# Feed-forward parts that multiply activations before they are normalised

## The chip, the cores and the metric

The kernel runs on one core of a Trainium2 chip. The metric is the device time of one execution in microseconds (us). PE is TensorE, PEld its weight loads, DVE is VectorE, ACT is ScalarE, POOL is GpSimd, SP is SyncE, which issues the loads from HBM.

## What is computed

Two blocks on 256 tokens of width 1024, each with two layers. The first block mixes 256 latent and 256 context tokens in layer 0; in layer 1 it computes outputs for the latent tokens alone. A layer of the first block ends in a modulated RMS norm and a feed-forward part, the block in an RMS norm. A layer of the second block is feed-forward, attention, feed-forward, each followed by a layer norm:

```python
def swiglu(u, w_ffn_in, w_ffn_out):
    gate, up = jnp.split(u @ w_ffn_in, 2, axis=-1)
    return (jax.nn.silu(gate) * up) @ w_ffn_out
...
    h = h + g2 * swiglu(modulate(rms_norm(h, norm2_w), sh2, sc2), w_ffn_in, w_ffn_out)
...
        x = layer_norm(ALPHA * x + 0.5 * swiglu_2(x, ffn1_w_in[l], ffn1_w_out[l]), ln_g[l, 0], ln_b[l, 0])
        mix = hybrid_mixer(x, cos, sin, mask, w_in[l], w_out[l], diff_lambda[l],
                           diff_subln_g[l], swa_sink[l], lambda_init)
        x = layer_norm(ALPHA * x + mix, ln_g[l, 1], ln_b[l, 1])
        x = layer_norm(ALPHA * x + 0.5 * swiglu_2(x, ffn2_w_in[l], ffn2_w_out[l]), ln_g[l, 2], ln_b[l, 2])
```

The hidden width is 2816, 22 tiles of 128.

## The kernel before

The program is written engine by engine, with semaphores between them; each engine runs its instructions in the order of the text. Activations lie transposed: `h` has 8 tiles (k = 0 to 7) of 128 features by tokens.

Weights come in **panels** of 128 x 2048 numbers (1 MB). Each panel is loaded into one of three `raw` buffers, then split into a high part `whi` (ACT, L569) and a rest `wlo` (L578: DVE takes 1280 of the 2048 columns, POOL 768). Activations are split the same way, into `xh` and `xl`. A product is three fp32r matmuls (L601 to L603): high x high, high weight x low, low weight x high. Every engine calls `step(p)` when it comes to panel p, and this splits panel p + 2; ACT's split waits until PE has used panel p - 1, whose buffer it takes.

A **feed-forward part** (`ffn`) has 33 panels. An input panel holds the gate and up weights of one hidden tile: 2 x 8 x 3 = 48 matmuls of 256 columns into one PSUM bank (bank 4 or 5; gate in columns 0 to 255, up in 256 to 511). An output panel holds two hidden tiles: 48 matmuls (L987 to L989) that accumulate into banks 0 to 3, which PE sets to zero at the start of the part (L962: 3 x 4 matmuls of 512 bf16 columns). Two input panels stand ahead of a loop whose body is input, input, output, input, input, output; a single output panel ends the part. An output panel takes the two tiles before the last two. For each tile ACT applies Silu to the gate (`sg`, L1838), DVE multiplies with up (`hidf`, L2522), ACT makes the high half (`hidh`, L1840), and DVE the low half (`hidl`, L2524).

There are seven parts. Two are in layer 0 of the first block. The five others, in the order of time: `("ffn", 1, 0)` after the output projection of layer 1; `ffn1` of layer 0 after the final norm (`"final"`); `ffn2` of layer 0 after the attention layer's projection (`("out2", 0)`); `ffn1` of layer 1 after `ffn2`; `ffn2` of layer 1 after `("out2", 1)`. They are called the first to the fifth part below.

Between two stages the norm stands on the path. For a layer norm PE sums `h` with a matrix of ones (L1523, 8 calls, two records each), ACT copies the mean, DVE subtracts it, ACT squares (L636), PE sums the squares (L628), ACT takes the root (L641), DVE the reciprocal (L652) and multiplies (L2937), ACT and DVE make the two halves (L2164, L2942), and PE starts the first tile, one k after the other. An RMS norm is the same without means. In the last loop turn of the first part DVE also computes the angles and lambda scalars of the second block (L2469 to L2500).

Of the kernel before, what the change touches and what calls it, by code (L numbers as in the profile page):

```python
# [21 lines left out]
P = 128  # L22
D, KD = 1024, 8
S, T = 256, 512
L = 2
# [17 lines left out]
PAR = {}  # L43
# [86 lines left out]
def program(nc, a, out, known):  # L130

    signals = {}
    with ExitStack() as stack:
# [36 lines left out]
        hid_hi, hid_lo = sem("hid_hi"), sem("hid_lo")  # L170
        gate_ready, merged = sem("gate_ready"), sem("merged")
# [143 lines left out]
        ytok2, _ = at(y_at + 14 * S * 4, "ytok2", [P, 2, D])  # L315
        ed, o = at(o, "ed", [P, 2, T])
        rc, o = at(o, "rc", [P, 2, S])
        sqs, o = at(o, "sqs", [P, 2, P])
        top = max(top, o)

        f2, _ = at(y_at, "f2", [P, 14, S])
        assert top <= nc.sbuf_usable_end, (top, nc.sbuf_usable_end)
# [333 lines left out]


# [120 lines left out]
        def _(pe):  # L778
# [176 lines left out]
            def ffn(tag, p0, t0, ops, last=False, fresh=None, evacuated=None, mids=None):  # L955

                fh, fl, cols = ops

# [4 lines left out]
                if evacuated is None:  # L963
# [15 lines left out]
                def output(p, per, it, pair_end, step, s_, final=False):  # L979
# [3 lines left out]
                    for j in range(2):  # L983
                        for n in range(8):
                            w0 = 1024 * j + P * n
                            dst = bank[n // 2][:, S * (n % 2):S * (n % 2) + S]
                            pe.matmul(dst, hi[:, w0:w0 + P], hidh[:, s_, j, :], start=False, stop=False, skip_group_check=True)  # L987
                            pe.matmul(dst, hi[:, w0:w0 + P], hidl[:, s_, j, :], start=False, stop=False, skip_group_check=True)  # L988
                            m = pe.matmul(dst, lo[:, w0:w0 + P], hidh[:, s_, j, :], start=False, stop=False, skip_group_check=True)  # L989
                            if final and j == 1 and n in (1, 3, 5):  # L990
                                m.then_inc(*pe_done.tick((tag, "acc", n // 2)))
                    m.then_inc(panel_used, 1)
# [11 lines left out]
                hidden(0, p0, 0, 0, t0, 0, fresh)  # L1004
                hidden(1, p0 + 1, 0, 0, t0 + 1, 0)
                if evacuated is not None:
                    pe.wait_ge(*dve_done.at(evacuated))
                    zero_banks()
# [2304 lines left out]
```

## Time and profile before

| | |
|---|---|
| median of 3 runs | 2973.78 us (2956.91 to 2979.4) |
| profiled execution | 2975.17 us, span of the instructions 2973.4 us |
| PE busy | 2815.5 us of the span |
| DVE, ACT, POOL busy | 1386.2, 1236.2, 1122.3 us |
| granted clock of TensorE, mean | 0.979 of full |

A matmul's record overlaps the next one's, so a busy PE is read from the spacing of starts, not from durations.

### The profile page before, as it was taken

What the parts mean: (1) busy time and instruction counts of PE and PEld (TensorE: products, weight loads), DVE (VectorE), ACT (ScalarE), POOL (GpSimd) and SP (SyncE); (2) the same over time, 40 slices, a digit from 0 to 9 for tenths busy, and PEclk for the clock granted to TensorE, in tenths of its full rate; (3) what the DMA queues carried; (4) which work ended last, traced back from release to release, by engine and by line L of the source; (5) the groups of instructions that cost most, each with busy time, mean ns of one, the idle gap of its engine ahead of it and who ended that gap; (6) DMA issues with size and microseconds to landing.
All of it is one profiled execution on the core that took longest, in us unless ns stands there. A gap on an engine that the chain in (4) does not pass through costs nothing. (4 is left out here: it accounts for less than half of the span.)

```text
span 2973.4 us, 53484 instructions
## 1 busy us (share of the span) xinstructions
PE 2815.5 (95%) x20993; PEld 2515.8 (85%) x20993; DVE 1386.2 (47%) x2415; ACT 1236.2 (42%) x1822; POOL 1122.3 (38%) x461
## 2 busy tenths in 40 slices
PE   7999999999999999899999998999889999988998
PEld 5667777788899999685889998998779989977898
DVE  4453543433633535536455435434754353466433
ACT  3321133433444545322455444444544444454443
POOL 1002021122455554110335454454526555543553
PEclk9998999999999999999999999999999999999999
DMA  6562352333466665210446565564326656622463
GB/s 221 175 215 79 114 135 86 82 95 106 144 197 184 184 190 169 65 56 18 111 105 188 167 185 170 155 184 142 106 65 199 194 155 187 198 86 86 143 187 96
DMA packets 574896, 417.92 MB, mean 141 GB/s; under 512 B 36694, under 2 KB 552476, under 8 KB 574748
## 3 DMA queue, kind: packets, MB, share of 16 engines
q1 hardware_dynamic: 574748, 415.88, 47.6%
q8 instruction: 101, 1.65, 0.2%
q14 instruction: 47, 0.39, 0.0%
HBM read 414.78 MB, written 2.88 MB: 140 GB/s over the span
## 5 line engine op out<-in xcount | busy, mean ns | idle before, releaser
L578 POOL TENSOR_TENSOR wlo<-raw,whi 128x768 fp32r<-128x768 f32 (+2 forms) x357 | 1022.7, 2867 | 1614.1 <-ACT whi L569 1613.6
L601 PE MATMUL psum<-xh_n,whi 128*128 128x256 f32 (+2 forms) x2880 | 828.2, 288 | 26.9 <-DVE rtmp L2958 8.9
L578 DVE TENSOR_TENSOR wlo<-raw,whi 128x1280 fp32r<-128x1280 f32 (+2 forms) x357 | 539.0, 1510 | 617.3 <-ACT whi L569 616.7
L602 PE MATMUL psum<-xl_n,whi 128*128 128x256 f32 (+2 forms) x2880 | 814.1, 283 | 0.0
L603 PE MATMUL psum<-xh_n,wlo 128*128 128x256 f32 (+2 forms) x2880 | 813.8, 283 | 0.0
L569 ACT ACTIVATE whi<-raw 128x2048 fp32r<-128x2048 f32 (+2 forms) x357 | 650.6, 1823 | 314.5 <-PE psum L989 151.1
L601 PEld LDWEIGHTS psum<-xh_n,whi 128*128 128x128 f32 (+1 forms) x2880 | 546.3, 190 | 57.6 <-issue 27.5
L603 PEld LDWEIGHTS psum<-xh_n,wlo 128*128 128x128 f32 (+1 forms) x2880 | 544.4, 189 | 4.0
L602 PEld LDWEIGHTS psum<-xl_n,whi 128*128 128x128 f32 (+1 forms) x2880 | 543.4, 189 | 3.7
L987 PE MATMUL psum<-hidh,whi 128*128 128x256 f32 x1232 | 343.1, 278 | 0.7 <-DVE hidl L2524 0.7
L989 PE MATMUL psum<-hidh,wlo 128*128 128x256 f32 x1232 | 342.9, 278 | 0.0
L988 PE MATMUL psum<-hidl,whi 128*128 128x256 f32 x1232 | 342.9, 278 | 0.0
L987 PEld LDWEIGHTS psum<-hidh,whi 128*128 128x128 f32 x1232 | 232.9, 189 | 1.0 <-issue 1.0
L1838 ACT ACTIVATE sg<-psum 128x256 f32<-128x256 f32 x154 | 59.2, 385 | 416.1 <-PE psum L603 416.0
L989 PEld LDWEIGHTS psum<-hidh,wlo 128*128 128x128 f32 x1232 | 232.0, 188 | 0.0
L988 PEld LDWEIGHTS psum<-hidl,whi 128*128 128x128 f32 x1232 | 231.3, 188 | 0.0
L2522 DVE TENSOR_TENSOR hidf<-sg,psum 128x256 f32<-128x256 f32 x154 | 64.8, 420 | 257.4 <-ACT sg L1838 257.2
L601 PE MATMUL psum<-xh,whi 128*128 128x512 f32 (+2 forms) x424 | 158.1, 373 | 3.1 <-DVE xl L2854 3.1
L603 PE MATMUL psum<-xh,wlo 128*128 128x512 f32 (+2 forms) x424 | 154.1, 363 | 0.0
L602 PE MATMUL psum<-xl,whi 128*128 128x512 f32 (+2 forms) x424 | 154.0, 363 | 0.0
L2524 DVE TENSOR_TENSOR hidl<-hidf,hidh 128x256 fp32r<-128x256 f32 x154 | 71.1, 462 | 74.6 <-ACT hidh L1840 74.6
L1840 ACT ACTIVATE hidh<-hidf 128x256 fp32r<-128x256 f32 x154 | 64.4, 418 | 97.2 <-DVE hidf L2522 97.2
(358 smaller groups left out, 4419.1 us busy)
## 6 DMA issues: line engine op xcount, KB each, us to landing
raw<-in_ffn_w_in SPq DMA_DIRECT2D x176, 512.0 KB
raw<-in_w_in SPq DMA_DIRECT2D x136, 512.0 KB
raw<-in_w_ffn_in SPq DMA_DIRECT2D x132, 512.0 KB
raw<-in_w_mod SPq DMA_DIRECT2D x96, 512.0 KB
raw<-in_ffn_w_out SPq DMA_DIRECT2D x88, 512.0 KB
raw<-in_w_ffn_out SPq DMA_DIRECT2D x66, 512.0 KB
raw<-in_w_out SPq DMA_DIRECT2D x40, 512.0 KB
raw<-in_w_a_o SPq DMA_DIRECT2D x16, 256.0 KB
```

The costliest lines, as they stand in the source:

```text
L569: act.activation(whi[slot][:, 0:size], raw[r % 3][:, 0:size], ACT.Copy).then_inc(hi_ready, 1)
L578: eng.tensor_tensor(wlo[slot][:, c0:c1], raw[raw_at[p0] % 3][:, c0:c1], whi[slot][:, c0:c1].bitcast(F32), ALU.subtract).then_inc(sem_, 1)
L601: pe.matmul(dst, sh, mh, start=start and n == 0, stop=False, skip_group_check=True)
L602: pe.matmul(dst, sh, ml, start=False, stop=False, skip_group_check=True)
L603: last = pe.matmul(dst, sl, mh, start=False, stop=n == len(pairs) - 1, skip_group_check=True)
L987: pe.matmul(dst, hi[:, w0:w0 + P], hidh[:, s_, j, :], start=False, stop=False, skip_group_check=True)
L988: pe.matmul(dst, hi[:, w0:w0 + P], hidl[:, s_, j, :], start=False, stop=False, skip_group_check=True)
L989: m = pe.matmul(dst, lo[:, w0:w0 + P], hidh[:, s_, j, :], start=False, stop=False, skip_group_check=True)
L1838: act.activation(sg[:, c, :], bank[4 + c][:, 0:S], ACT.Silu).then_inc(silu_done, 1)
L1840: act.activation(hidh[:, s_, c, :], hidf[:, c, :], ACT.Copy).then_inc(hid_hi, 1)
L2522: dve.tensor_tensor(hidf[:, c, :], sg[:, c, :], bank[4 + c][:, S:2 * S], ALU.mult).then_inc(hid_done, 1)
L2524: dve.tensor_tensor(hidl[:, s_, c, :], hidf[:, c, :], hidh[:, s_, c, :].bitcast(F32), ALU.subtract).then_inc(hid_lo, 1)
```

## The change

In the five parts PE multiplies a vector that is scaled by feature but not yet by token. `xd` holds, for each k, 256 columns of h times the norm's weight (high part, and low part 384 columns further on), and two columns of the norm's shift, so matmuls have 258 columns; the second part has no shift and keeps 256. Gate and up go to banks of their own (4 and 5, 6 and 7). The sums of squares are taken by one-column matmuls between those of the first tile; the reciprocal roots are put on a diagonal, one matmul with ones turns them into a row on all partitions, and ACT copies it to `stat`. DVE multiplies gate and up with `stat` when it takes them out of PSUM (`gs`, `us`); the shift's product enters as a bias of Silu and as a scalar in `hidf`. The normalised `h` that the residual needs is made by DVE after the first and the second tile.

Further: banks are cleared by one matmul of 32 columns each, once; the last output panel runs bank by bank, and the means of a layer norm are put between its matmuls (or those of the attention layer's projection); the q panel of the gated linear attention of layer 1 computes 256 tokens, not 512; POOL adds the shift to `h` four panels later.

```diff
+            def raw_operands(tag):
+
+                for k in range(8):
+                    wait_raw(act, tag, k)
+                    act.activation(xd[:, k, 0:S], h[:, k, 0:S], ACT.Copy, scale=raw_factor(tag, k)).then_inc(*act_done.tick((tag, "hi", k)))
+                    act_square(act, tag, k, h[:, k, 0:S], slice(0, S))
+                act.activation(tiny[:, 6:7], eps[:, 0:1], ACT.Sqrt)
...
+                def raw_steps(c, p, half, ks):
...
+                        pe.matmul(dst, w[0][:, k, :], xr_h, start=k == 0, stop=False, skip_group_check=True)
+                        pe.matmul(dst, w[1][:, k, :], xr_h, start=False, stop=False, skip_group_check=True)
+                        m = pe.matmul(dst, w[0][:, k, :], xr_l, start=False, stop=k == 7, skip_group_check=True)
...
+                def raw_entry():
...
+                    for k in range(8):
+                        pe.wait_ge(*dve_done.at((fresh, "lo", k)))
+                        raw_steps(0, p0, 0, (k,))
+                        m = raw_steps(0, p0, 1, (k,))
...
+                        pe.wait_ge(*act_done.at((fresh, "sq", k)))
+                        for t in range(2):
+                            m = pe.matmul(bank[0][:, t:t + 1], squares_at(k, slice(0, S))[0][:, P * t:P * t + P], ones[:, 0:1],
+                                          start=k == 0 and t == 0, stop=k == 7, skip_group_check=True)
...
+                    raw_steps(1, p0 + 1, 0, range(8))
+                    pe.wait_ge(*dve_done.at((fresh, "diag")))
+                    pe.matmul(bank[1][:, 0:S], ones[:], sq[:, 0, 0:S], start=True, stop=True).then_inc(*pe_done.tick((fresh, "rows")))
+                    raw_steps(1, p0 + 1, 1, range(8)).then_inc(panel_used, 1)
+                    pe.wait_ge(*act_done.at((fresh, "stat")))
+                    clear_banks()
...
+                    if tz is not None:
+                        pe.wait_ge(up_scaled, it * step + (t - t0 + tz - 1))
+                        raw_steps(c, p, 0, range(8))
+                        raw_steps(c, p, 1, range(8)).then_inc(panel_used, 1)
+                        return
...
+                def scaled_hidden(c, p, per, it, t, nstep, s_):
...
+                    dve.wait_ge(panel_used, it * per + (p + 1))
+                    if biased:
+                        dve.tensor_copy(tiny[:, 2 * c:2 * c + 2], psum[:, 4 + 2 * c:6 + 2 * c, S])
+                    dve.tensor_tensor(gs[:, c, :], bank[4 + 2 * c][:, 0:S], stat[:, 0:S], ALU.mult).then_inc(gate_scaled, 1)
+                    dve.tensor_tensor(us[:, c, :], bank[5 + 2 * c][:, 0:S], stat[:, 0:S], ALU.mult).then_inc(up_scaled, 1)
...
+                        dve.scalar_tensor_tensor(hidf[:, c, :], us[:, c, :], tiny[:, 2 * c + 1:2 * c + 2], sg[:, c, :], ALU.add, ALU.mult
+                                                 ).then_inc(hid_done, 1)
...
-                    dve.tensor_tensor(hidf[:, c, :], sg[:, c, :], bank[4 + c][:, S:2 * S], ALU.mult).then_inc(hid_done, 1)
...
-                g = generic_f(tg, p0, [(0, P), (P, P)], 8, 256, slice(0, T), xh, xl, 0)
+                g = generic_f(tg, p0, [(0, P), (P, P)], 8, 256, slice(0, TM), xh, xl, 0)
```

PE's order at the start of the fifth part, before (`whi` and `wlo` are the weights' halves, `xh_n` and `xl_n` the operand's):

```order
L603 MATMUL psum<-xh_n,wlo_57 128x256
L1523 MATMUL psum<-h,ones 128x256 [waits dve_done] x8
L628 MATMUL psum<-sq,ones 128x256 [waits act_done] x8
L962 MATMUL psum<-zero,ones 128x512 [waits act_done]
L962 MATMUL psum<-zero,ones 128x512 x11
L601 MATMUL psum<-xh_n,whi_52 128x256 [waits hid_done,lo_ready_pool,dve_done,lo_ready,hi_ready]
L602 MATMUL psum<-xl_n,whi_52 128x256
L603 MATMUL psum<-xh_n,wlo_55 128x256
L601 MATMUL psum<-xh_n,whi_52 128x256 [waits dve_done]
```

and after (L1111 are the means, L1026 the one-column sums; the first two k of the first tile):

```order
L609 MATMUL psum<-xh_n,wlo_57 128x256
L1111 MATMUL psum<-h,ones 128x256 [waits dve_done] x2
L1008 MATMUL psum<-xd,whi_52 128x258 [waits up_scaled,lo_ready_pool,dve_done,lo_ready,hi_ready]
L1009 MATMUL psum<-xd,wlo_55 128x258
L1010 MATMUL psum<-xd,whi_52 128x258
L1008 MATMUL psum<-xd,whi_52 128x258
L1009 MATMUL psum<-xd,wlo_55 128x258
L1010 MATMUL psum<-xd,whi_52 128x258
L1026 MATMUL psum<-ones,sq 128x1 [waits act_done]
L1026 MATMUL psum<-ones,sq 128x1
L1008 MATMUL psum<-xd,whi_52 128x258 [waits dve_done]
```

Six of the eight means have moved ahead of the projection's last 12 matmuls; the sums stand inside the first tile, and the twelve filler matmuls are gone.

DVE's order in the loop of a part, two tiles and the splits, before:

```order
L578 TENSOR_TENSOR wlo_56<-raw_50,whi_53 128x1280 [waits hi_ready]
L2519 ISA
L2521 REGISTER_ALU [waits silu_done]
L2522 TENSOR_TENSOR hidf<-sg,psum 128x256 [waits hid_hi]
L2524 TENSOR_TENSOR hidl<-hidf,hidh 128x256 [waits hid_hi]
L576 REGISTER_ALU
L578 TENSOR_TENSOR wlo_57<-raw_51,whi_54 128x1280 [waits hi_ready]
```

and after, one tile of a part that has a shift:

```order
L584 TENSOR_TENSOR wlo_56<-raw_50,whi_53 128x1280 [waits hi_ready]
L2673 ISA
L2674 REGISTER_ALU [waits silu_done]
L2676 COPY tiny<-psum 128x2 [waits panel_used]
L2677 TENSOR_TENSOR gs<-psum,stat 128x256
L2678 TENSOR_TENSOR us<-psum,stat 128x256
L2679 REGISTER_ALU
L2680 REGISTER_ALU [waits up_scaled]
L2684 SCALAR_TENSOR_TENSOR hidf<-us,tiny,sg 128x256 [waits hid_hi,silu_done]
L2699 TENSOR_TENSOR hidl<-hidf,hidh 128x256 [waits hid_hi]
L582 REGISTER_ALU
L584 TENSOR_TENSOR wlo_57<-raw_51,whi_54 128x1280 [waits hi_ready]
```

DVE waits for PE's tile itself now and has three more instructions ahead of `hidf`.

DVE's order at the end of the first part, after (`h<-psum,mod,h` evacuates; before, the eight of them stood together):

```order
L584 TENSOR_TENSOR wlo_57<-raw_51,whi_54 128x1280 [waits hi_ready]
L2622 SCALAR_TENSOR_TENSOR lam<-ast 128x1 [waits act_done]
L2624 TENSOR_SCALAR subln<-subln 128x128
L2622 SCALAR_TENSOR_TENSOR lam<-ast 128x1
L2624 TENSOR_SCALAR subln<-subln 128x128
L3098 SCALAR_TENSOR_TENSOR h<-psum,mod,h 128x256 [waits pe_done]
L3098 SCALAR_TENSOR_TENSOR h<-psum,mod,h 128x256
L2649 SCALAR_TENSOR_TENSOR xd<-h,par,xd 128x256 [waits act_done]
L3098 SCALAR_TENSOR_TENSOR h<-psum,mod,h 128x256 [waits pe_done]
L2649 SCALAR_TENSOR_TENSOR xd<-h,par,xd 128x256 [waits act_done]
```

The low halves now go between the evacuations, behind the same split and scalars.

## Rows read from the trace of the kernel before

**Rows 1.** The page, busy us and share of the span.

```profile
PE 2815.5 (95%) x20993; PEld 2515.8 (85%) x20993; DVE 1386.2 (47%) x2415; ACT 1236.2 (42%) x1822; POOL 1122.3 (38%) x461
```

**Rows 2.** PE by windows: length, busy (count), granted clock, DMA share, GB/s.

```profile
1296.00:1306.00 10.00, 10.00 (x44) 1.00 0.34 105
2260.00:2360.00 100.00, 100.00 (x885) 1.00 0.65 189
2780.00:2880.00 100.00, 100.00 (x852) 1.00 0.65 189
```

**Rows 3.** PE's timeline, entry of the fifth part: start, length, engine, line.

```profile
2749.69 0.28 PE L603 MATMUL psum<-xh_n,wlo 128*128 128x256 f32 x1
2749.81 3.62 PE L1523 MATMUL psum<-h,ones 128*128 128x256 f32 x16
...
2759.10 2.76 PE L962 MATMUL psum<-zero,ones 128*128 128x512 bf16 x12 [0.57 <-ACT stat L641]
...
2788.12 0.28 PE L987 MATMUL psum<-hidh,whi 128*128 128x256 f32 x1
```

**Rows 4.** PE and DVE timelines, entry of the second part, and a window's clock.

```profile
1845.37 0.28 PE L989 MATMUL psum<-hidh,wlo 128*128 128x256 f32 x1
1852.88 5.26 PE L628 MATMUL psum<-sq,ones 128*128 128x256 f32 x16 [7.23 <-ACT sq L636]
...
1887.23 0.28 PE L987 MATMUL psum<-hidh,whi 128*128 128x256 f32 x1
...
1836.87 0.43 DVE L2524 TENSOR_TENSOR hidl<-hidf,hidh 128x256 fp32r<-128x256 f32 x1 [0.48 <-ACT hidh L1840]
...
1846.92 1.76 DVE L2498 SCALAR_TENSOR_TENSOR lam<-ast 128x1 f32<-128x1 f32 x1
...
1848.94 3.21 DVE L2910 SCALAR_TENSOR_TENSOR h<-psum,mod,h 128x256 f32<-128x256 f32 x8
...
1850.00:1856.00 6.00, 3.12 (x8) 2.52 (x8) 2.15 (x6) 2.35 (x7) 0.00 (x0) 0.50 0.45 169
```

**Rows 5.** PE's timeline, entry of the first part.

```profile
1646.49 0.28 PE L603 MATMUL psum<-xh_n,wlo 128*128 128x256 f32 x1
...
1681.55 0.28 PE L987 MATMUL psum<-hidh,whi 128*128 128x256 f32 x1
```

**Rows 6.** PE's timeline, entries of the third and the fourth part.

```profile
2205.44 0.28 PE L603 MATMUL psum<-xh_n,wlo 128*128 128x256 f32 x1
...
2243.13 0.28 PE L987 MATMUL psum<-hidh,whi 128*128 128x256 f32 x1
...
2400.78 0.28 PE L989 MATMUL psum<-hidh,wlo 128*128 128x256 f32 x1
...
2438.52 0.28 PE L987 MATMUL psum<-hidh,whi 128*128 128x256 f32 x1
```

**Rows 7.** The chain that ended last, entry of the fifth part.

```profile
2753.47 0.39 ACT rtmp L2156
...
2761.38 0.52 ACT xh_n L2164
...
2761.93 0.48 DVE xl_n L2942
2762.41 0.40 DVE h L2937
```

**Rows 8.** PE's timeline, one-column matmuls early in the program.

```profile
78.86 1.84 PE L1030 MATMUL psum<-ones,sq 128*128 128x1 f32 x16
```

**Rows 9.** ACT's, DVE's and POOL's timelines, one tile of the fifth part.

```profile
2833.55 0.39 ACT L1838 ACTIVATE sg<-psum 128x256 f32<-128x256 f32 x1 [3.74 <-PE psum L603]
...
2834.75 1.90 ACT L569 ACTIVATE whi<-raw 128x2048 fp32r<-128x2048 f32 x1
...
2836.68 1.49 DVE L578 TENSOR_TENSOR wlo<-raw,whi 128x1280 fp32r<-128x1280 f32 x1 [1.38 <-ACT whi L569]
...
2836.72 3.15 POOL L578 TENSOR_TENSOR wlo<-raw,whi 128x768 fp32r<-128x768 f32 x1 [3.68 <-ACT whi L569]
```

More of the change, by code:

```diff
@@ L1014, in ffn, with layer_means @@
                 output(p0 + 32, 0, 0, t0 + 22, 0, 0, final=True)
+            def layer_means(tg, ks):
+                for k in ks:
+                    pe.wait_ge(*dve_done.at((tg, "u", k)))
+                    pe.matmul(bank[ln_bank(tg)][:, 0:S], ones[:], h[:, k, 0:S], start=k == 0, stop=k == 7
+                              ).then_inc(*pe_done.tick((tg, "mean", k)))
             site = [0]
@@ L1512, in _ @@
                 end("pe", ("ffn", l))
-            stage(pe, "pe", "block2", ("ffn", L - 1))
-            pe_sum(pe, "final", 8, 6, slice(0, S))
-            end("pe", "block2")
-            prev = "block2"
-            def layer_norm_pe(tg):
-                for k in range(8):
-                    pe.wait_ge(*dve_done.at((tg, "u", k)))
-                    pe.matmul(bank[ln_bank(tg)][:, 0:S], ones[:], h[:, k, 0:S], start=k == 0, stop=k == 7
-                              ).then_inc(*pe_done.tick((tg, "mean", k)))
-                pe_sum(pe, tg, 8, ln_bank(tg) + 1, slice(0, S))
+            prev = "final"
             for l in range(L):
@@ L1706, in _ @@
                     tg = ("ffn%d" % which, l)
-                    ffn(tg, base[tg], FT * site[0], (xh, xl, slice(0, S)), last=which == 2 and l == L - 1,
-                        fresh=prev if prev != "block2" else "final")
+                    last = which == 2 and l == L - 1
+                    ffn(tg, base[tg], FT * site[0], (None, None, None), last=last, fresh=prev, tz=FT * (site[0] - 2), means=True)
                     site[0] += 1
-                    layer_norm_pe(tg)
+                    if which == 1 or last:
+                        pe_sum(pe, tg, 8, ln_bank(tg) + 1, slice(0, S))
                     end("pe", tg)
@@ L2143, in _, with layer_mean_act @@
                 end("act", ("ffn", l))
-            stage(act, "act", "block2", ("ffn", L - 1))
-            act_squares(act, "final", [h[:, k, 0:S] for k in range(8)], slice(0, S), 0, D, 6, lambda k: None)
-            for k in range(8):
-                act.wait_ge(*dve_done.at(("final", "t", k)))
-                act.activation(xh[:, k, 0:S], h[:, k, 0:S], ACT.Copy).then_inc(*act_done.tick(("final", "hi", k)))
-            end("act", "block2")
-            prev = "block2"
-            def layer_norm_act(tg, last=False):
+            raw_operands("final")
+            prev = "final"
+            def layer_mean_act(tg):
                 act.wait_ge(*pe_done.at((tg, "mean", 7)))
@@ L3148, in _ @@
                 end("pool", ("ffn", l))
-            end("pool", "block2")
             prev = None
```

271 lines of the change are left out of this document (201 added, 70 removed).

## The prediction

> **What bounds the kernel now.** I read the page's busy line first. TensorE (PE) is busy for 2815.5 of 2973.4 us [rows 1], so time can only leave the program where PE's work shrinks or where PE stands still. The count of matmuls in quiet windows comes next [rows 2]; one or two of each count only reach in over an edge. 852 in 100 us in one feed-forward part is 0.1176 us a matmul, 885 in another is 0.1133, and 44 in 10 us is 0.233 for matmuls of 512 columns. So inside a part PE issues without a hole, and there is nothing to win there. PE's timeline at the change from one stage to the next shows the holes. The last useful matmul before the fifth changed part starts at 2749.69, and the first output panel (L987) starts at 2788.12 [rows 3], 38.3 us after PE went over to the means. The four input panels between need 4 x 48 x 0.1176 = 22.6 us. The other 15.7 us are 3.5 us of means, 3.7 us of sums, 12 filler matmuls, and waits for statistics and operands. At the other changed parts the same stretch is 41.7 us (1845.49 to 1887.23) [rows 4], 34.9 us (1646.61 to 1681.55) [rows 5], 37.6 us and 37.6 us [rows 6]. All five stretches lie wholly on the path.
>
> **Entry into a part, by its pieces.** PE now starts on the first tile when operand k = 0 is there. For each of 8 k it does 6 matmuls of 258 columns and 2 matmul calls with one column. Calls in full fp32 are two records each, and 16 such records take 1.84 us with the tail of the last, 0.112 each [rows 8]. So one k costs 6 x 0.118 + 4 x 0.112 + about 0.1 for the change of number format = 1.25 us, and the first tile 9.9 us. The second tile costs 5.7 us, plus the row of reciprocals (two records, 0.45) and four clears, 6.2 us. Two more input panels are 11.35 us. Sum: 27.5 us from the first matmul to the first output panel.
>
> I take 0.6 us of waiting on top. PE ends the second tile 6.3 us after the first. VectorE (DVE) gets the copied row at about 4.2 us, splits a panel for 1.5 us, and needs 0.85 us to scale gate and up, so `up_scaled` comes at 6.6 us; four residual multiplies of 0.4 us then delay the next split, and GpSimd's half of it (3.15 us [rows 9]) ends about 0.3 us late. So an entry costs 28.1 us from its first matmul.
>
> Where means come first (the third to the fifth part) PE waits from the mean to the first operand: the mean's copy 0.39, a subtraction 0.42 (as a multiply of that size), the high half 0.52, the low half 0.48 [rows 7] and four hand-overs, 2.0 us. DVE's 0.8 us and ScalarE's (ACT) 0.9 us per k stay below PE's 1.25 us. At both ends of the attention layer only 6 means can be done early; the last two wait for the last evacuation, and the mean is ready 4.0 us after the start of the old stretch. After a feed-forward part it is ready at 3.7 us, as before, since the total of means is the same.
> - Fifth part: 4.0 + 2.0 + 28.1 = 34.1 against 38.3, -4.2 us.
> - Third: at 0.1133 a matmul, 33.3 against 37.6, -4.3 us. Fourth: 33.0 against 37.6, -4.6 us.
> - First: the operands of the earlier k are made while PE still multiplies, so PE starts at once: 28.1 against 34.9, -6.8 us.
> - Second: here it does not. In the last turn of the part before, DVE also makes the angles and the lambda scalars. It starts to evacuate h at 1848.94, 3.5 us after PE's last matmul [rows 4], and the order in the program keeps those scalars ahead of h. The change gives this DVE four tiles with two more multiplies, 3.8 us; part of that falls into its gaps, and I take 1.7 us as the shift. With h, h and one low half, the first operand is there 6.5 us after PE's end. PE idle for that long had its clock at half (0.50 granted between 1850 and 1856, after the idle time of 7.23 us [rows 4]), so I add 2 us for the first matmuls. 6.5 + 28.0 + 2 = 36.5 against 41.7, -5.2 us.
>
> Sum of the entries: -25.1 us.
>
> The Trainium skill speaks against the second tile's timing: SBUF: State Buffer, Who interferes with whom, says that a DVE instruction with two SBUF inputs and a GpSimd instruction that reads SBUF lock each other out for a whole instruction. `hidf` used to read one factor from PSUM and now reads both from SBUF, so by that rule it can stand behind GpSimd's split. The trace agrees as to the splits: the two start within 0.04 us, DVE's takes 1.49 and GpSimd's 3.15 us [rows 9]. By it the sum would stay as it is as long as the loop below has slack.
>
> **Inside the parts.** Two extra columns: (0.233 - 0.1176) / 256 = 0.45 ns each [rows 2], 0.9 ns a matmul. Four of the five parts have them (the second has no shift), 4 x 22 x 48 = 4224 matmuls, 3.8 us; the entries above hold 0.7 of it, +3.1 us remain.
>
> The new wait is DVE's for PE's finished tile, and ACT's for the scaled gate; behind them stand the panel splits on both engines. Loop of a tile now: sg starts at 2833.55 and DVE's split ends at 2838.17 [rows 9], 4.6 us. The column copy (0.1), the gate's multiply (0.42) and a hand-over make it 5.2 us; up's multiply runs beside sg. An output panel takes 1.90 + 1.49 + 0.05 = 3.4 us. Two tiles and an output panel: 13.8 us, with a blocked `hidf` of 0.3 us each 14.4, against PE's 3 x 5.64 = 16.9 us (16.3 at the quicker pace). The panel's GpSimd half is ready some 7 us after PE left the tile and is needed after 11.3. So I cost this at nothing; without the cover each microsecond beyond 16.9 costs 50 us in the 50 pairs of tiles.
>
> **Beside the parts.** GLA's q panel of the second layer goes from 512 to 256 columns: 48 x (0.233 - 0.1176) = -5.5 us, PE has no wait there, so I take all of it (bounds 0 and -5.5). Clearing four banks with 32 instead of 512 columns in the two parts of the first layer: 8 x (0.23 - 0.03) = -1.6 us (12 of the wide ones take 2.76 us [rows 3]). The means between output matmuls are the same work.
>
> Sum: -25.1 + 3.1 - 5.5 - 1.6 = **-29.1 us**. The profiled execution took 2975.2 us (span 2973.4), 1.4 above the median of 2973.8; so about **2946 us**. What no row shows: one-column calls inside an fp32r stream (between 0 and +0.35 us a k, if each hand-over leaves PE waiting: 0 to +14 us), the entry of the second part (-13.7, if PE could start at once, to 0), the price of columns 257 and 258 (0.9 ns, or the 7.2 ns of a whole step of 16 columns), a tile's loop (0 to blocked, below).
>
> **Rivals.**
> 1. *The second entry is clean.* DVE takes the extra multiplies in its gaps and h does not wait: PE would wait 4 instead of 6.5 us and keep its clock. DVE ends the last tile's `hidl` at 1837.30 [rows 4], and the final output panel (48 matmuls before 1845.49) needs it at 1839.8; this gap of 2.5 us speaks for it, the scalars ahead of h speak against. About 8 us less at most: 2938.
> 2. *The hand-over paces the entry.* Operands come from three engines, and at 1.6 us a k the entries give 14 us back: 2960. Against it, 0.8 to 0.9 us of DVE and ACT work a k.
> 3. *Two columns cost a step.* 4224 x 7.2 ns = 30 instead of 3.8 us: 2972. For it: 256 columns take 0.1133 us, 6.6 ns above 256 periods of 2.4 GHz, so something besides columns is paid. Against it: the rows of 256 and of 512 columns show no price of an odd length, only that 512 cost twice 256 within 1%.
> 4. *The pace of the parts changes.* The same code runs at 0.1176 in some parts and at 0.1133 in others at a granted clock of 1.00 [rows 2], so this is no property of the edit. By my count of starts four of the seven parts run at the quicker pace. All seven slow: 4 x 1584 x 4.3 ns = +27, 2973. All fast: three parts, -21, 2925.
> 5. *Slower.* The tile's loop passes PE's. Its place is DVE's queue in the loop body: `hidf` and `hidl` have two SBUF inputs, and GpSimd's split ends 1.66 us after DVE's. If three of the four in a pair of tiles stand behind it for all of that: 13.8 + 5.0 = 18.8 us against 16.9, +1.9 x 50 = +95: 3041. It decides from 16.9 us on, which is two such blocks in a pair. Against it: GpSimd's split ends about 0.3 us after the next tile's `hidf` could start, not 1.66, unless DVE runs late.
>
> **How the numbers follow.** Forecast (entries as summed, loop covered) 0.60, own range 2933 to 2959; rival 1 0.10; rival 2 0.08; rival 3 0.05; rival 4 slow 0.05, fast 0.07; rival 5 0.05. The range reaches from the fast pace to the slow one and rival 3: 2925 to 2974. About 1% is what a measurement of this kernel can tell from no change, here 29.7 us, 2944. Half of the forecast's cases, rival 1 and the fast pace lie below it: 0.30 + 0.10 + 0.07 = 0.47 faster. Rival 5 is slower: 0.05. The rest, 0.48, is the same within 1%.
>
> **What the profile after would show.** From the last useful matmul to the first output panel: about 28 us (first part), 36 (second), 33 to 34 (others). 32 one-column records in each entry, 0.112 apart, and k steps of about 1.25 us. PE waits for `us` or `up_scaled` once per entry, under 1 us, and never in the loop. DVE's h of the second entry starts 5 us after PE's end, and the clock falls there. Spacing of 258-column matmuls 0.9 ns over 0.1133 or 0.1176. Wrong if matmuls in the loop show idle time before them that DVE ends, if a k takes 1.6 us, or if spacing grows by 7 ns.

## The result, and the profile after

| | before | after |
|---|---|---|
| median, same chip | 2973.21 us (2956.91 to 2979.4, 4 runs) | 3009.12 us (3000.59 to 3010.81, 4 runs) |
| ratio | | 1.0127, 95% interval 1.0088 to 1.0165 |
| profiled execution, span | 2973.4 us | 3006.6 us |
| granted clock, mean | 0.979 | 0.961 |

The change makes the kernel slower, by some 36 us (26 to 49 by the interval), where 29 us of gain were forecast. The page of the changed kernel, PE's busy line and the granted clock in 40 slices (answers to [rows 1]; before, every slice but the fourth reads 9):

```profile
PE 2849.7 (95%) x21043; PEld 2564.8 (85%) x21043; DVE 1497.5 (50%) x2729; ACT 1246.5 (41%) x1841; POOL 1114.9 (37%) x461
...
PEclk9989899899999999999999998999989989999899
```

The busy share is still 95%: the lost time doesn't show as idle time. It shows as slices of 8 in the clock's line, late in the program, where before had none. (The 8s in the first quarter stand ahead of the five parts and make about a third of the 0.018 between the two mean clocks; experiment 9 comes back to them.) PE's timeline at the entries of the third, fourth and fifth part (start, length, line; L1008 to L1010 multiply the raw operand, L1026 are the one-column sums, L1071 is the first output panel):

```profile
2210.27 0.28 PE L609 MATMUL psum<-xh_n,wlo 128*128 128x256 f32 x1
...
2213.86 0.36 PE L1008 MATMUL psum<-xd,whi 128*128 128x258 f32 x1 [2.08 <-DVE xd L2649]
...
2249.83 0.36 PE L1071 MATMUL psum<-hidh,whi 128*128 128x256 f32 x1
...
2417.64 0.28 PE L1073 MATMUL psum<-hidh,wlo 128*128 128x256 f32 x1
...
2457.67 0.36 PE L1071 MATMUL psum<-hidh,whi 128*128 128x256 f32 x1
...
2783.76 0.36 PE L1008 MATMUL psum<-xd,whi 128*128 128x258 f32 x1 [2.08 <-DVE xd L2649]
...
2784.91 0.36 PE L1008 MATMUL psum<-xd,whi 128*128 128x258 f32 x1
...
2788.84 0.56 PE L1008 MATMUL psum<-xd,whi 128*128 128x258 f32 x1
...
2790.98 0.56 PE L1008 MATMUL psum<-xd,whi 128*128 128x258 f32 x1
...
2819.72 0.36 PE L1071 MATMUL psum<-hidh,whi 128*128 128x256 f32 x1
```

PE waits 2.08 us for the first operand, as forecast (2.0). The first k of the fifth part takes 1.15 us (2783.76 to 2784.91), the fourth 2.14 (2788.84 to 2790.98): the same matmuls, nearly twice as long, and no wait between them. The windows of the changed kernel at the second to the fifth entry say why (length, busy and count for PE, PEld, DVE, ACT, POOL, then granted clock, DMA share, GB/s):

```profile
1853.50:1877.40 23.90, 20.81 (x97) 20.84 (x98) 8.71 (x23) 11.41 (x22) 2.94 (x2) 0.50 0.13 45
2215.30:2232.30 17.00, 17.00 (x82) 17.00 (x81) 4.01 (x12) 7.17 (x15) 1.82 (x1) 0.50 0.00 0
2423.60:2440.60 17.00, 17.00 (x82) 17.00 (x81) 3.53 (x11) 8.14 (x14) 1.82 (x1) 0.50 0.00 0
2785.40:2802.40 17.00, 17.00 (x81) 17.00 (x81) 3.82 (x12) 6.97 (x14) 1.82 (x1) 0.50 0.00 1
```

The granted clock is 0.50 (1.2 GHz) for 24 and three times for 17 us. In the three PE is busy without a hole; the first begins in PE's wait and holds 20.8 us of work. Busy time at half clock is about half lost, as an estimate (20.8 + 3 x 17) / 2 = 35.9 us. The same place in the kernel before, fifth entry:

```profile
2759.00:2776.00 17.00, 15.19 (x102) 12.12 (x103) 12.46 (x21) 9.81 (x14) 5.30 (x4) 1.00 0.09 22
```

There PE is idle for 1.8 us of the 17 and keeps 1.00 (2.4 GHz). Before, only the first and the second entry fell to 0.50. The second had 3.1 us of PE work in it [rows 4], the first this:

```profile
1658.10:1661.50 3.40, 3.40 (x13) 3.17 (x14) 2.81 (x7) 1.87 (x5) 0.00 (x0) 0.50 0.00 0
```

After the change the first entry keeps its clock. PE waits there for only 0.78 us and then runs the same one-column sums.

The second entry starts late for the reason forecast, a little more so. PE and DVE after:

```profile
1849.10 0.28 PE L1073 MATMUL psum<-hidh,wlo 128*128 128x256 f32 x1
1856.59 0.55 PE L1008 MATMUL psum<-xd,whi 128*128 128x256 f32 x1 [7.21 <-DVE xd L2649]
...
1851.48 1.49 DVE L584 TENSOR_TENSOR wlo<-raw,whi 128x1280 fp32r<-128x1280 f32 x1 [2.07 <-ACT whi L575]
1852.89 1.76 DVE L2622 SCALAR_TENSOR_TENSOR lam<-ast 128x1 f32<-128x1 f32 x1
...
1854.91 0.86 DVE L3098 SCALAR_TENSOR_TENSOR h<-psum,mod,h 128x256 f32<-128x256 f32 x2
```

DVE comes to h 5.8 us after PE's last matmul started (forecast 5), behind a split and the lambda scalars.

Then the pace inside parts. Between the first L1008 and the first L1071 of a loop turn stand 96 matmuls. Starts in the third part (258 columns), then in the second (256), after:

```profile
2306.72 0.28 PE L1008 MATMUL psum<-xd,whi 128*128 128x258 f32 x1
...
2318.31 0.28 PE L1071 MATMUL psum<-hidh,whi 128*128 128x256 f32 x1
...
1916.34 0.28 PE L1008 MATMUL psum<-xd,whi 128*128 128x256 f32 x1
...
1927.22 0.28 PE L1071 MATMUL psum<-hidh,whi 128*128 128x256 f32 x1
```

11.59 us / 96 = 120.8 ns against 10.88 / 96 = 113.3 ns. Two columns cost 7.5 ns, not 0.9. Nor do the waits by line (total, times, longest) show a loop that waits; PE's waits for `hidl`, the operand of the output panels, are three, 1.4 us in all. The second row below is the means waiting at the end of the second, third and fourth part:

```profile
PE psum L1008 <- DVE xd L2649: 14.2, 5, 7.2
...
PE psum L1111 <- DVE h L3231: 3.6, 3, 1.2
```

### The profile page after: what moved, and what is told of

The parts are those of the page before. It is cut to its first block and busy times, and to the rows that moved or that the text cites. A ratio compares the mean times of both kernels' runs of the same rounds, so it can differ in the third digit from the quotient of the medians.

```text
span 3006.6 us, 54170 instructions
## 1 busy us (share of the span) xinstructions
PE 2849.7 (95%) x21043; PEld 2564.8 (85%) x21043; DVE 1497.5 (50%) x2729; ACT 1246.5 (41%) x1841; POOL 1114.9 (37%) x461
## 5 line engine op out<-in xcount | busy, mean ns | idle before, releaser
L1008 PE MATMUL psum<-xd,whi 128*128 128x258 f32 (+1 forms) x1760 | 514.5, 292 | 16.1 <-DVE xd L2649 14.2
L1009 PE MATMUL psum<-xd,wlo 128*128 128x258 f32 (+1 forms) x1760 | 506.9, 288 | 0.0
L1010 PE MATMUL psum<-xd,whi 128*128 128x258 f32 (+1 forms) x1760 | 506.7, 288 | 0.0
L1008 PEld LDWEIGHTS psum<-xd,whi 128*128 128x128 f32 x1760 | 345.0, 196 | 19.1 <-issue 18.9
L607 PE MATMUL psum<-xh_n,whi 128*128 128x256 f32 (+2 forms) x1120 | 331.3, 296 | 19.0 <-DVE rtmp L3148 8.9
L1009 PEld LDWEIGHTS psum<-xd,wlo 128*128 128x128 f32 x1760 | 345.0, 196 | 0.1
L1010 PEld LDWEIGHTS psum<-xd,whi 128*128 128x128 f32 x1760 | 344.9, 196 | 0.0
L1071 PE MATMUL psum<-hidh,whi 128*128 128x256 f32 x1232 | 343.0, 278 | 1.7 <-DVE hidl L2699 1.4
L608 PE MATMUL psum<-xl_n,whi 128*128 128x256 f32 (+2 forms) x1120 | 321.3, 287 | 0.0
L609 PE MATMUL psum<-xh_n,wlo 128*128 128x256 f32 (+2 forms) x1120 | 321.2, 287 | 0.0
L607 PEld LDWEIGHTS psum<-xh_n,whi 128*128 128x128 f32 (+1 forms) x1120 | 213.7, 191 | 40.0 <-issue 21.3
L1071 PEld LDWEIGHTS psum<-hidh,whi 128*128 128x128 f32 x1232 | 231.6, 188 | 2.9 <-issue 2.4
L609 PEld LDWEIGHTS psum<-xh_n,wlo 128*128 128x128 f32 (+1 forms) x1120 | 213.0, 190 | 3.2
L608 PEld LDWEIGHTS psum<-xl_n,whi 128*128 128x128 f32 (+1 forms) x1120 | 213.1, 190 | 3.0
```

Of the source, the lines that this page charges most:

```text
L607: pe.matmul(dst, sh, mh, start=start and n == 0, stop=False, skip_group_check=True)
L608: pe.matmul(dst, sh, ml, start=False, stop=False, skip_group_check=True)
L609: last = pe.matmul(dst, sl, mh, start=False, stop=n == len(pairs) - 1, skip_group_check=True)
L1008: pe.matmul(dst, w[0][:, k, :], xr_h, start=k == 0, stop=False, skip_group_check=True)
L1009: pe.matmul(dst, w[1][:, k, :], xr_h, start=False, stop=False, skip_group_check=True)
L1010: m = pe.matmul(dst, w[0][:, k, :], xr_l, start=False, stop=k == 7, skip_group_check=True)
```

## Experiments

Theory A: the clock falls because PE's work at the entry has become light or is missing (idle time, 32-column clears), where the kernel before had full 512-column filler matmuls. Theory B: it is the one-column matmuls inside the first tile. Theory C: the loss that matters is that of the two columns.

**1. Fillers in the waits.** The changed kernel with 512-column bf16 matmuls into an unused bank ahead of the first operand (PE also waits there for the last tile's `us`, which this bank held):

```diff
+                    for _ in range(33 if fresh == "final" else 0 if fresh[0] == "norm2" else 9):
+                        pe.matmul(bank[7], ones_b, zeros, start=True, stop=True)
                     for k in range(8):
                         pe.wait_ge(*dve_done.at((fresh, "lo", k)))
```

> The changed kernel, and before the first tile of the second to the fifth part PE runs filler matmuls (512 bf16 columns of zeros into bank 7): 33 in the second, 9 in the third to the fifth, about the time for which it stood idle there (7.2 and 2.1 us). Theory A (the idle time before the entry takes the clock, and nothing fills it as the removed clears did): the four entries run at full clock, the windows at half clock of 17.1 us (three times) and 23.9 us go or shrink to 7 us, and the time falls by 24 to 34 us against the changed kernel, to about 2975 to 2985. Theory B (the one-column matmuls hold the clock down or pull it down by themselves): the clock still falls inside the first tile and stays down for 10 us or more; the gain is under 12 us, 2997 or more.

Measured: 2973.81 us (2960.75 to 2983.37, 10 runs), ratio to before 1.0009 (0.9986 to 1.0032), where the changed kernel had 1.0127: about 35 us are back (22 to 48 by the two intervals). Windows of this kernel at the second, third and fourth entry:

```profile
1848.00:1872.00 24.00, 23.52 (x194) 22.04 (x192) 15.49 (x35) 15.10 (x28) 5.09 (x2) 1.00 0.29 89
2202.00:2219.00 17.00, 16.95 (x136) 15.83 (x134) 8.79 (x23) 10.16 (x24) 1.82 (x1) 1.00 0.01 2
2402.00:2419.00 17.00, 16.95 (x136) 15.80 (x135) 9.01 (x23) 11.54 (x25) 1.83 (x1) 1.00 0.00 1
```

136 records in 17 us instead of 82 (a few of them fillers), at a clock of 1.00, with the one-column matmuls still there. So these don't bring the clock down by themselves. The half clock was the loss, and filling the wait removes it.

**2. No one-column matmuls.** The squares are summed by one call of 256 columns per k, with ones as weights; the root and the reciprocal are taken on the whole row, so the diagonal and its matmul go; no fillers:

```diff
-                        for t in range(2):
-                            m = pe.matmul(bank[0][:, t:t + 1], squares_at(k, slice(0, S))[0][:, P * t:P * t + P], ones[:, 0:1],
-                                          start=k == 0 and t == 0, stop=k == 7, skip_group_check=True)
+                        m = pe.matmul(bank[0][:, 0:S], ones[:], squares_at(k, slice(0, S))[0], start=k == 0, stop=k == 7, skip_group_check=True)
```

> The changed kernel without fillers, but the sums of squares are 256-column matmuls (ones stationary, the squares moving, one call for each k) in place of two one-column calls; the root and the reciprocal are then taken on the whole row, and the diagonal and its matmul go. PE's time for a k is the same within 0.05 us (two records of 0.22 against four of 0.11). Theory A (idle time takes the clock, and whatever follows, it needs long to come back): the half-clock windows stay at 17 us, time within 8 us of 3009. Theory B (one-column matmuls keep it down): the clock falls as before, at the start of the entry, but comes back after some 7 us, as it did after idle stretches of the kernel before; 4 entries x 5 us = 20 us less, about 2989.

Measured: 2970.01 us (2963.41 to 2984.24, 10 runs), ratio 1.001 (0.9989 to 1.003), again about 35 us below the changed kernel where theory B had 20. The half-clock windows that this kernel has at its entries:

```profile
1846.80:1857.00 10.20, 5.79 (x23) 5.46 (x24) 8.77 (x20) 5.17 (x13) 2.45 (x1) 0.50 0.40 125
2406.60:2410.00 3.40, 3.40 (x15) 3.22 (x14) 2.92 (x8) 2.33 (x7) 0.00 (x0) 0.50 0.00 0
2761.60:2765.00 3.40, 3.40 (x14) 3.06 (x14) 2.86 (x8) 2.44 (x8) 0.00 (x0) 0.50 0.02 5
```

The clock still falls at three entries, since the wait is still there, but comes back after 3.4 us (10.2 at the second, which holds 4.4 us of idle time). In the changed kernel it stayed down for the whole first tile, and came back 3 to 4 us after the last one-column matmul. So both theories hold a part: the clock falls with the wait, and the one-column matmuls keep it down. This holds in most executions, not in all: of the 16 entries with a wait in the four profiles that have one-column sums and no fillers (after, experiments 3, 7 and 10), 13 lose the clock until after the sums and two not at all, and at the second entry of experiment 7 it came back while the sums still ran. What decides it is not shown. The 32-column clears of theory A have no part in it: they come after the second tile, when the clock is back.

**3. No shift.** The changed kernel with 256 columns everywhere:

```diff
-            return S if tag == "final" else S + 2
+            return S
```

> The changed kernel with the norm's shift left out of all five parts: 256 columns in every part, no bias of Silu, no column copy. Its result lacks the shift in gate and up. Theory C (the two columns cost a step of 7.5 ns a matmul, 4224 matmuls): input matmuls of 0.113 us, 31 us less than the changed kernel, 2978. Theory D (the extra 7 ns come from something else in the new parts: banks, DVE's reads, the pace that changes from part to part): spacing stays near 0.120, and the time within 8 us of 3009.

Measured: 2977.53 us (2969.11 to 3001.3, 10 runs), ratio 1.0033 (1.0003 to 1.0062), some 28 us below the changed kernel by the ratios (13 to 42 by the two intervals). This kernel leaves the shift out, so it is a probe and not a kernel to use. Windows of the third entry, the first and the second part:

```profile
2215.00:2232.00 17.00, 17.00 (x83) 17.00 (x83) 3.85 (x12) 7.00 (x14) 1.81 (x1) 0.51 0.00 0
1700.00:1800.00 100.00, 100.00 (x885) 100.00 (x884) 51.99 (x71) 44.47 (x45) 59.04 (x19) 1.00 0.64 194
1900.00:2000.00 100.00, 100.00 (x851) 100.00 (x851) 48.36 (x66) 43.22 (x42) 57.93 (x19) 1.00 0.65 195
```

The clock is lost as before, and the parts run at 113 ns (885 in 100 us) or 117.5 (851). The columns and the clock are two losses of about the same size. If they add up, a kernel without both stands at 1.0127 - 0.0118 (fillers) - 0.0094 (columns) = 0.9915; experiment 11 tests that.

**4. The q panel alone.** The kernel before with the last line of the change:

```diff
-                g = generic_f(tg, p0, [(0, P), (P, P)], 8, 256, slice(0, T), xh, xl, 0)
+                g = generic_f(tg, p0, [(0, P), (P, P)], 8, 256, slice(0, TM), xh, xl, 0)
```

> The kernel before with one part of the change alone: the q panel of layer 1's gated linear attention at 256 instead of 512 columns (and DVE's two operations on it). All theories: 48 matmuls at half length, -5.5 us against the kernel before, 2968; less if that stage is bound by DVE further on.

Measured: 2958.25 us (2952.5 to 2970.33, 10 runs), ratio 0.9964 (0.9946 to 0.9981): 5.6 to 16 us of gain. The forecast's 5.5 lies just outside. Its profile has all five parts at 113.3 ns between matmuls; whether its executions drew quick parts by luck (experiment 9) isn't settled.

**5. Two columns in one product of three.** Experiment 1 with

```diff
-                        pe.matmul(dst, w[1][:, k, :], xr_h, start=False, stop=False, skip_group_check=True)
-                        m = pe.matmul(dst, w[0][:, k, :], xr_l, start=False, stop=k == 7, skip_group_check=True)
+                        pe.matmul(dst[:, 0:S], w[1][:, k, :], xr_h[:, 0:S], start=False, stop=False, skip_group_check=True)
+                        m = pe.matmul(dst[:, 0:S], w[0][:, k, :], xr_l[:, 0:S], start=False, stop=k == 7, skip_group_check=True)
```

> The changed kernel with the fillers of the first experiment, and with the two shift columns in the first of the three products alone (high weights times high activations): its two columns now hold the high and the low half of the shift, their sums are added on evacuation, and the product of the low weights with the shift is left out (a part in some thousands of the shift's term). The other two products of each tile have 256 columns. If each matmul with 258 columns costs 7.5 ns more than one with 256 at the fast pace (120.8 against 113.3 ns in the changed kernel), two thirds of 4224 matmuls give back 2816 x 7.5 = 21 us: about 2953 us. If the columns cost what lies between 258 columns and the slow pace of 256 (120.8 - 117.8 = 3.0 ns), 8.5 us: about 2965 us. If one wide matmul in three already sets the pace of the stretch, nothing: 2974 us.

Measured: 2970.37 us (2962.52 to 2977.54, 10 runs), ratio 1.0011 (0.9993 to 1.0028): nothing is gained over experiment 1. Starts of 96 input and then 48 output matmuls, third part:

```profile
2305.36 0.28 PE L1008 MATMUL psum<-xd,whi 128*128 128x258 f32 x1
...
2316.66 0.28 PE L1073 MATMUL psum<-hidh,whi 128*128 128x256 f32 x1
...
2322.32 0.28 PE L1008 MATMUL psum<-xd,whi 128*128 128x258 f32 x1
```

11.30 us / 96 = 117.7 ns, and 5.66 / 48 = 117.9 for the output panel. One wide matmul in three costs 4.4 ns on each of the three where the part would run at 113.3 (13 ns for a wide one), and nothing where it would run at 117.8. That the input panels stand at 117.7 here could still be the slow pace itself; experiment 6 has them at 117.8 beside quick output panels. The 3 ns that this form gives back against 120.8 (4 x 1056 x 3 = 12.7 us) didn't reach the median: in this profile all four parts with a shift drew the slow pace for their output panels (in that of experiment 1 one of four).

**6 and 12. All mends.** Experiment 5 with the sums of experiment 2, the rotary and lambda scalars moved behind the low halves at the second entry, and 20 fillers there:

```diff
-                if tag == ("ffn", L - 1, 0):
-                    rotary_scalars()
...
                     if l == L - 1:
                         raw_lo("final", 7)
+                        rotary_scalars()
```

> The former kernel with the squares summed by 256-column matmuls and no diagonal step, the rotary scalars moved behind the evacuation that the second entry waits for, and so 20 fillers there instead of 33 (9 at each other entry). If the columns give back 21 us and the second entry's wait of 7.2 us falls to 2 to 4: 2945 to 2950 us, below the kernel before with the q panel alone (2958). If the columns give nothing back: about 2968. If the moved scalars then delay the second entry by another way (the store of them is waited for in the attention behind): 2955 to 2975.

Measured: 2950.51 us (2946.52 to 2962.2, 6 runs), ratio 0.9945 (0.9924 to 0.9965). The wait at the second entry hardly shrank: 4.49 us of fillers and 1.54 us of idle time stand there, against 7.21, where 2 to 4 were expected. Input panels again at 117.8 ns, output panels at 113.4:

```profile
2303.34 0.28 PE L1008 MATMUL psum<-xd,whi 128*128 128x258 f32 x1
...
2314.65 0.28 PE L1069 MATMUL psum<-hidh,whi 128*128 128x256 f32 x1
...
2320.09 0.28 PE L1008 MATMUL psum<-xd,whi 128*128 128x258 f32 x1
```

> The kernel with all mends, once more with more rounds, for its interval: 0.990 to 0.997 of the kernel before (2936 to 2958 us) if the first measurement stands. If that one drew fast parts by luck, 0.997 to 1.001. In its profile the four parts with two columns in one product stand at 117.8 ns on input matmuls whatever their output matmuls do (113.3 or 117.8).

The second measurement gave 2959.02 us (2948.44 to 2964.35, 12 runs), ratio 0.9966 (0.9945 to 0.9988). So this form is faster than the kernel before, by 4 to 23 us over both intervals, and than the changed one. It is not shown to be faster than the kernel before with the q panel alone (0.9964).

**7. Sixteen columns.** The changed kernel with `S + 16`:

```diff
-            return S if tag == "final" else S + 2
+            return S if tag == "final" else S + 16
```

> The changed kernel with 16 shift columns instead of two in all three products (272 columns). A straight line by columns from 113.3 ns at 256 (0.42 ns each at 2.4 GHz) plus a fixed price of 6.7 for leaving 256: 126.7 ns a matmul, 4224 x 5.9 = +25 us on the changed kernel: about 3034. If the price is a step at 16 columns: 120.8 as with two, and no change: 3009. If it is 3.7 ns a column, as the two columns were: 173 ns, +220 us: 3229.

Measured: 3018.44 us (3017.46 and 3019.42, 2 runs), ratio 1.0174 (1.0152 to 1.0196).

```profile
2311.72 0.29 PE L1008 MATMUL psum<-xd,whi 128*128 128x272 f32 x1
...
2323.56 0.28 PE L1071 MATMUL psum<-hidh,whi 128*128 128x256 f32 x1
```

11.84 / 96 = 123.3 ns: 14 more columns cost 2.5 ns, where the first two cost 7.5. That is neither a straight line from 256 nor a flat step of 16 columns. The two points fit a price for leaving 256 columns and 0.18 ns (2.5 / 14) for each column; a third width was not run. The fourth entry kept its clock in this profile, and the second got it back after 10.2 us, at 1864.9, with one-column sums still to come (the last starts at 1870.9):

```profile
1864.90:1871.00 6.10, 6.10 (x56) 6.10 (x55) 0.48 (x1) 4.52 (x6) 0.64 (x1) 1.00 0.01 3
```

**8. The kernel before with fewer fillers.** 4 of the 12 filler matmuls stay at each entry:

```diff
-                    for _ in range(3):
+                    for _ in range(1):
                         zero_banks()
```

> The kernel before with 4 instead of 12 filler matmuls at the entry of each feed-forward part with a norm ahead of it (the clearing of the four banks stays, twice of three times goes). If it is the fillers and their 512-column matmuls that kept the clock up there, half-clock stretches of 7 to 17 us appear at the entries, each worth 3.5 to 8.5 us: 2985 to 3005 us. If the clock fell in the changed kernel by its one-column matmuls alone, no new half-clock stretch shows and the time stays at 2968 to 2973 us, since the fillers lay in a wait.

Measured: 2970.53 us (2957.04 to 2976.77, 10 runs), ratio 1.0018 (1.0002 to 1.0035). Half-clock windows at the second to the fifth entry:

```profile
1842.50:1852.70 10.20, 6.06 (x14) 4.90 (x15) 3.41 (x11) 4.28 (x9) 0.00 (x0) 0.50 0.31 103
2207.70:2211.10 3.40, 3.27 (x13) 3.04 (x14) 2.93 (x8) 1.87 (x5) 0.00 (x0) 0.50 0.00 0
2402.30:2409.10 6.80, 6.62 (x29) 6.25 (x28) 4.42 (x11) 4.97 (x7) 0.63 (x1) 0.50 0.01 2
2760.70:2764.10 3.40, 3.40 (x14) 2.88 (x13) 3.22 (x9) 2.04 (x4) 0.00 (x0) 0.50 0.00 0
```

With fewer fillers the clock falls at the third to fifth entry too, for 3.4 to 6.8 us instead of 17, and the price is about 5 us (0.6 to 10 by the interval), where 2985 us or more were expected. None of the three profiles with all twelve fillers (before, experiments 4 and 9) falls at these three entries. The fillers of the kernel before did hold the clock, and without one-column matmuls behind them the loss is short.

**9 and 10. Both kernels again.**

> The kernel before, unchanged, profiled once more. If each part's pace (113.3 or 117.8 ns between its matmuls) is a property of the program, the parts repeat it: first, second and fifth at 117.8, third and fourth at 113.3, span 2973. If it is drawn anew in each execution, some part changes its pace, and its length goes by 6.2 us (163.83 against 157.65), with the span by as much.

2972.05 us. Windows of 100 us in the first part and 40 us in the fourth:

```profile
1700.00:1800.00 100.00, 100.00 (x884) 100.00 (x884) 37.87 (x44) 44.50 (x45) 56.74 (x18) 1.00 0.66 194
2500.00:2540.00 40.00, 40.00 (x342) 40.00 (x341) 14.69 (x17) 17.31 (x18) 22.07 (x7) 1.00 0.58 173
```

In the first profile of this program the first, second and fifth part ran at 117.8 ns; in this one the fourth alone does (342 in 40 us) and the others at 113.3. The pace belongs to the execution and the part, not to the program. A part is 6.2 us longer at the slow one, and five draws span 31 us; this kernel's times spread over 30 (2954.18 to 2984.18 over 31 runs). They are not the only draw. Experiment 4 runs the code of the kernel before up to layer 1, and yet it stood at half clock for 27 us in layer 0, where the kernel before has full clock for most of the time:

```profile
525.40:552.70 27.30, 25.96 (x103) 20.48 (x101) 8.46 (x29) 10.46 (x27) 0.00 (x0) 0.50 0.18 44
524.90:552.20 27.30, 24.22 (x137) 19.11 (x138) 15.47 (x42) 17.79 (x41) 0.07 (x1) 0.94 0.26 66
```

(Experiment 4 first, then before.) The profile after has this stretch too, and those of experiments 6, 7 and 12; the others don't. So one profile against another holds some microseconds that the change has no part in.

> The changed kernel, unchanged, as a control beside the next two on one chip. If the clock lost at its entries is a property of the program, half-clock stretches of 17 to 24 us stand at the second to fifth entry again and the time is 3000 to 3011 us, 1.2 to 1.4% above the kernel before. If the loss was drawn in that one execution, some of them are gone and the time spreads down to 2975.

3004.08 us (3000.05 to 3007.07, 4 runs), ratio 1.0126 (1.0085 to 1.0166). Half-clock windows at the second, fourth and fifth entry; the third kept its clock:

```profile
1845.10:1869.00 23.90, 20.61 (x96) 20.64 (x97) 8.92 (x23) 11.42 (x22) 3.15 (x2) 0.50 0.13 45
2408.30:2428.80 20.50, 20.50 (x98) 20.50 (x98) 4.84 (x14) 9.38 (x18) 1.82 (x1) 0.50 0.00 1
2776.90:2794.00 17.10, 17.10 (x82) 17.10 (x81) 3.58 (x11) 6.80 (x13) 1.82 (x1) 0.50 0.00 1
```

**11. All mends, no shift.** Experiment 6 with the edit of experiment 3.

> The kernel with all mends, without the shift of the norms: its columns, halves and the addition on evacuation are left out, so every matmul of the four later parts has 256 columns (the result lacks the shift's term). If two columns in one product of three cost 4.5 ns a matmul where the part would run at 113.3 ns and nothing where it would run at 117.8, it is 0 to 19 us faster than the kernel with all mends, by the pace that its parts draw: 2932 to 2950, near 2940. If the columns cost nothing in this form, the same time: 2950. If the norm's bias instructions on the scalar and vector engine stood on the entry's path, 5 us more are gained at the entries, which the gaps ahead of the first panel would show.

Measured: 2938.29 us (2932.38 to 2956.71, 5 runs), ratio 0.989 (0.985 to 0.993). That is 0.0076, 23 us, below experiment 12 on the same chip. At most 4 x 1056 x 4.4 = 18.6 us of it is the columns' pace in one product of three; the rest is within the intervals. With the clock kept, the columns gone and the scalars moved, the un-normalised form with the q panel is worth 33 us (21 to 45), but this kernel leaves the shift out: it shows what the two losses cost, and is no version to use. The 0.9915 of experiment 3 lies within its interval, so nothing speaks against the two losses adding up.

## Why the prediction was wrong

**Entries.** Their geometry was right. Taken from the end of useful work to the first output panel, as in the prediction (where means were moved ahead of the last matmuls, their 0.2 us a record is added again: 12 records at the third and fifth part, 8 at the fourth), and with the clock's loss taken off (half of PE's busy time at 0.50):

| part | before | forecast | after, without the clock's loss | clock's loss |
|---|---|---|---|---|
| first | 34.9 | 28.1 | 29.0 | 0 |
| second | 41.7 | 36.5 (2 of it clock) | 34.3 | 10.4 |
| third | 37.6 | 33.3 | 33.3 | 8.5 |
| fourth | 37.6 | 33.0 | 33.0 | 8.5 |
| fifth | 38.3 | 34.1 | 33.3 | 8.5 |

The gain without the clock is 27.2 us, and the forecast's 25.1 held 2 us of clock loss, so the same. (Before held some clock loss as well, by the same estimate 1.7 us at the first entry and 1.6 at the second.) The k step was 1.15 us at full clock (forecast 1.25), the operand's wait 2.08 (2.0), `up_scaled` never waited for. That the sum fits so well is in part luck: eight shorter k steps save 0.8 us, and 258-column matmuls at 120.8 ns take 0.3 to 1.0 us back in the other three panels.

**The step that failed: "I add 2 us for the first matmuls", at the second entry alone.** The forecast took the clock as something that a 6.5 us wait costs once, and that comes back with work. The third to fifth entries were given no loss, and no rival had one. Measured: 35.9 us at four entries by the estimate above, and (20.6 + 20.5 + 17.1) / 2 = 29.1 at three in experiment 10. The 12 fillers were treated as work to be saved; experiment 8 shows that they held the clock (5 us when two thirds are taken away), and experiments 1 and 2 that either filling the wait or taking the one-column matmuls out ends the long loss. A hint could be read beforehand: the fillers of [rows 3] stand in the window 2759 to 2776, shown above, with 1.8 us of idle time and a clock of 1.00.

**Two columns.** The term of 0.9 ns, 3.8 us for 4224 matmuls, was mis-sized. It measured 7.5 ns at the quick pace and 3.0 at the slow one (13 to 32 us), about 28 us by experiment 3. The forecast had named spacing that grows by 7 ns as a sign of being wrong, and the sign came. This is the price of rival 3, which had a chance of 0.05 and by itself gave 2972. Its mechanism, a step of 16 columns, is not what experiment 7 shows. The slope between 256 and 512 columns was the wrong row: it can't tell a price that is paid for leaving 256. The Trainium skill (TensorE: Matmul & The Clock Gate, Back-to-back issue gap) would have misled in the same way: it gives N / 2.4 GHz + 2.5 ns for a matmul without the weight load between, so by an estimate 0.8 ns for two columns. It says itself that a stream of weight loads and matmuls keeps another pace, which it gives for 128 and 512 columns alone. The trace, of such a stream, says 7.5.

**Beside these.** The means between the last output matmuls wait for DVE's h, 3.6 us in three places, which "the same work" had at nothing. The q panel gave 5.6 to 16 us where 5.5 were forecast. The pace of the parts (rival 4) is drawn in each execution (experiment 9), as the forecast supposed; it widens the spread but decided nothing. DVE's loop (rival 5) is covered: the parts run at the pace of their matmuls, and no wait of PE for `us` stands in the profile. Yet what rival 5 feared does happen, in a third of the tiles. An `hidf` of the third part, and the split on POOL that runs when it starts:

```profile
2268.79 1.91 DVE L2684 SCALAR_TENSOR_TENSOR hidf<-us,tiny,sg 128x256 f32<-128x256 f32 x1 [0.25 <-ACT sg L1958]
...
2268.57 1.85 POOL L584 TENSOR_TENSOR wlo<-raw,whi 128x768 fp32r<-128x768 f32 x1
```

The instruction takes 1.91 us where most take 0.48. In this profile 36 of the 110 `hidf` of the five parts start while such a split runs, each takes over 0.6 us (0.66 to 1.91), and each ends 0.28 or 0.29 us after the split. In the kernel before, where `hidf` takes one factor from PSUM, 28 start beside a split and none takes over 0.42. So the lock of which the forecast spoke is seen here for `hidf` too; PE stood still for none of it but perhaps the 1.4 us for `hidl`.

**The sum.** Forecast -29.1; +34 for the clock (35.9 less the 2 foreseen), +24 for the columns (28 less 3.8), +3.6 for the means: +32.5. Measured +35.9, and +37.7 in experiment 10, whose profile has less clock loss (29.1 us), so the sum closes no better than the spread allows. Undoing both failed terms gives 0.989 (0.985 to 0.993, experiment 11), where the forecast without its columns is (2975.2 - 32.2) / 2975.2 = 0.9892. The closeness is luck in part, since experiment 11 also moves scalars and drops the diagonal.

## What to carry to other kernels

Before fillers or waits at the start of a stage are removed, read the granted clock there and ask what PE will do in the first microseconds instead: a gain of 5 us can cost 8.5 us of half clock, and PE's busy share won't show it. Price a matmul of a new shape by a matmul of that shape, since two columns more than 256 cost as much as 17 by the slope from 256 to 512. Where the same part shows two paces at full clock, compare sums over parts with the pace taken out, or many runs.

## What was unexpected of the hardware

- fp32r matmuls of 256 columns run at 113.3 or 117.8 ns at a granted clock of 1.00, constant through a part and drawn anew in each execution (experiments 4 and 9 against before). What draws it stays open.
- 258 columns: 120.8 ns, whichever pace the output panels beside them have; 272: 123.3 ns (experiment 7); 258 once in three: 117.8 on average (experiments 6 and 12).
- After a wait of 2.1 us, one-column fp32 matmuls between 256- or 258-column ones held the granted clock at 0.50 for 17 to 20.5 us with PE busy all through, at 10 of the 12 third to fifth entries of four profiles (after, experiments 3, 7 and 10); after 0.8 us or less, or behind fillers, the same matmuls ran at 1.00 (first entry, experiment 1). One 256-column call in their place let the clock return after 3.4 us at the fourth and fifth entry.
- `hidf` with both factors in SBUF, when it starts beside GpSimd's split, ends 0.28 or 0.29 us after that (36 of 36, after); with one factor in PSUM it keeps its 0.42 us (28 of 28, before).
